# Order of ScalarE's and VectorE's steps at the end of a SwiGLU FFN, in a decoder trunk on one Trainium2 core

## The chip, the cores and the metric

One NeuronCore of a Trainium2 chip runs the whole program. The metric is device time of one launch in microseconds (us). TensorE does the matmuls (PE in the profile), VectorE is DVE, ScalarE is ACT, GpSimd is POOL, SyncE is SP and issues the loads of the weights. Each engine runs its own instructions strictly in the order in which they are written, and waits for others by counting semaphores.

## The reference, cut to what matters

Four layers, each of them FFN, token mixer, FFN: twelve sub-layers, of which eight are FFNs of this form, with 256 tokens, a model width of 1024 and an inner width of 2816, in float32.

```python
def rmsnorm(x, g):
    x32 = x.astype(jnp.float32)
    y = x32 * lax.rsqrt(jnp.mean(x32 * x32, axis=-1, keepdims=True) + EPS)
    return (y * g.astype(jnp.float32)).astype(x.dtype)

def swiglu(x, wg, wu, wd):
    return (jax.nn.silu(x @ wg) * (x @ wu)) @ wd
...
        x = x + 0.5 * rmsnorm(swiglu(rmsnorm(x, g[0]), ffn1_wg[i], ffn1_wu[i], ffn1_wd[i]), g[1])
```

## The kernel before, in words

**Weights come as a stream of pieces** of 128 x 2048 floats (1 MB), in the order of their use. A piece passes through four hands. SP loads it into one of three buffers `raw` (L580). ScalarE's `high` (L1254) rounds it to the matmul's format in `w_high`, one of six places. VectorE's `low` (L1702) subtracts that from the piece and so makes the rest, `w_low`. TensorE then multiplies in three passes: high by high, high by low, low by high. The three `raw` buffers tie the end of this line to its beginning: SP loads piece p only when `low` of piece p - 3 is done. It waits for `piece_split`, a semaphore that `low` raises, so the order of VectorE's `low` steps is the order and the time of the loads.

**An FFN** has 33 pieces, w0 to w0 + 32, where w0 is its first. The inner width is 22 blocks of 128. For a block TensorE makes gate and up products (`block`), ScalarE makes silu of the gate (`silu_of`, L1300), and VectorE multiplies it by up (`times_up`, L1775). The down projection works in chunks of two blocks. Chunks 0 to 8 are done with seven products in place of eight (`seven`), which need sums of the result to be put together at the end. Chunks 9 and 10 (blocks 18 to 21) are done plainly (`chunk`). Pieces w0 + 29 and w0 + 30 hold the weights of blocks 20 and 21, w0 + 31 and w0 + 32 those of chunks 9 and 10. Pieces from w0 + 33 on belong to the next sub-layer. The constants are BLOCKS = 22, SEVENS = 9, FFN_PIECES = 33, CHUNKS = 11.

**TensorE's order at the end of an FFN**: block 19, the last of the seven products of chunk 8 (L774 to L778), block 20, block 21, then chunk 9 for the first 128 tokens, chunk 10 for the first 128 tokens, and after that the second 128 tokens with two groups of transposes of the next sub-layer's input among them (L649). Block 20 waits until block 19 has been multiplied by `times_up`; block 21 until `first_part_out` (L1343) has copied a partial output out of its bank; chunk 9 until `join` and `chunk_low` are done; chunk 10 until `h_low` of block 21 (L1866) is done; the transposes wait for the normalised input, xn (L1750).

**ScalarE's order there**: `high(w0 + 30)`, silu of block 18, `high(w0 + 31)`, `high(w0 + 32)`, silu of block 19, `first_part_out`, `chunk_high` (L1337), `high` of w0 + 33 and w0 + 34, silu of block 20, `h_high` of it (L1348), `high(w0 + 35)`, silu of block 21, `h_high` of it, `high(w0 + 36)`, then the squares of the output for the norm (`square_y`, L1263).

**VectorE's order there**: `times_up` of block 18, `low` of w0 + 30 and w0 + 31, `times_up` of block 19, `low(w0 + 32)`, `join` (L1849 to L1855, five additions that put the partial outputs together; they need ScalarE's `first_part_out`), `low(w0 + 33)`, `times_up` of block 20, `chunk_low` (L1841), `h_low` of block 20, `low(w0 + 34)`, `times_up` of block 21, `join_second`, `h_low` of block 21, `join_second`, `low(w0 + 35)`, then the joint between sub-layers: `gain_y` (L1721), `update_x` (L1738), `pre_norm` (L1750).

At the end of the eighth and last FFN no further pieces follow, so `high` and `low` of w0 + 33 and up do nothing there.

Of the kernel before, what the change touches and what calls it, by code (L numbers as in the profile page):

```python
# [163 lines left out]
def build(nc, x_in, gains, first_gain, stream, gate_w, gate_b, conv_k, ident_in, rope_in, att_mask_in, ml_mask_in,  # L164
          tri_in, out):
    with ExitStack() as ctx:
# [18 lines left out]
        def high_of(p):  # L185
            return w_high[:, p % RING, place(p)]
# [240 lines left out]
        def w_of(sub):  # L427
            return BASE[sub]

        def ffn_no(sub):  # L430
            return KINDS[:sub].count("ffn")
# [37 lines left out]
        def half_of(c, first, last):  # L469

            return slice((c % 2) * 1024 + first * P, (c % 2) * 1024 + last * P)

        def free_part(sub, c):

            return w_of(sub) + down_piece(c) + 1
# [764 lines left out]
        def _(act):  # L1240
# [5 lines left out]
            def high(p, turn=0):  # L1246

                if p >= PIECES:
                    return
                act.wait_ge(raw_landed[p % RAW], 16 * (p // RAW + 1) + 32 * turn)  # L1250
                if p >= RING:

                    act.wait_ge(piece_used, p - RING + 1 + RING * turn)
                nc.scalar.activation(high_of(p)[:, :], raw[:, p % RAW, :], ACT.Copy).then_inc(piece_high, 1)  # L1254
# [78 lines left out]
            def chunk_high(sub, c):  # L1333

                act.wait_ge(h_ready, BLOCKS * ffn_no(sub) + 2 * c + 2)
                act.wait_ge(piece_used, free_part(sub, c - 2))
                nc.scalar.activation(oT_hi_flat[:, half_of(c, 0, 4)], h_all[:, c % 2, 0:4, :].rearrange("p a b -> p (a b)"),  # L1337
                                     ACT.Copy).then_inc(hT_high_done, 1)

            def first_part_out(sub):  # L1340

                act.wait_ge(piece_used, free_part(sub, SEVENS - 1))
                nc.scalar.activation(sums[:, 0:HALF], ps[:, 1, :], ACT.Copy).then_inc(first_copied, 1)  # L1343
# [88 lines left out]
            def ffn(sub):  # L1432
                w0 = w_of(sub)

                def unit(c, turn=0):
                    p = w0 + block_piece(2 * c + 2)
                    silu_of(sub, 2 * c + 2, turn=turn)
                    high(p + 4, turn)
                    corners_high(sub, c + 1, turn)
                    silu_of(sub, 2 * c + 3, turn=turn)  # L1440
                    sums_high(sub, c + 1, turn)
                    seven_h_high(sub, c + 1, turn)
                    high(p + 6, turn)

                silu_of(sub, 1)
                if sub == 0:
                    high(w0 + 4)
                corners_high(sub, 0)
                if sub == 0:
                    silu_of(sub, 2)  # L1450
                sums_high(sub, 0)
                high(w0 + 6)
                if sub:
                    silu_of(sub, 2)
                silu_of(sub, 3)
                copy_hT(sub, 0)
                seven_h_high(sub, 0)
                corners_high(sub, 1)
                silu_of(sub, 4)
                copy_hT(sub, 1)  # L1460
                sums_high(sub, 1)
                seven_h_high(sub, 1)
                high(w0 + 8)
                if sub == 0:
                    load_gains(sub)
                high(w0 + 9)
                silu_of(sub, 5)
                seven_h_high(sub, 2)
                corners_high(sub, 2)
                sums_high(sub, 2)  # L1470
                high(w0 + 11)
                with act.Fori(0, (SEVENS - 3) // 2) as turn:
                    unit(2, turn)
                    unit(3, turn)
                high(w0 + 30)
                silu_of(sub, BLOCKS - 4)
                high(w0 + 31)
                high(w0 + 32)
                silu_of(sub, BLOCKS - 3)
                first_part_out(sub)  # L1480
                chunk_high(sub, SEVENS)
                high(w0 + FFN_PIECES)
                high(w0 + FFN_PIECES + 1)
                silu_of(sub, BLOCKS - 2)
                h_high(sub, BLOCKS - 2)
                high(w0 + FFN_PIECES + 2)
                silu_of(sub, BLOCKS - 1)
                h_high(sub, BLOCKS - 1)
                high(w0 + FFN_PIECES + 3)
# [203 lines left out]
        def _(dve):  # L1693
# [3 lines left out]
            def low(p, turn=0):  # L1697

                if p >= PIECES:
                    return  # L1700
                dve.wait_ge(piece_high, p + 1 + RING * turn)
                nc.vector.tensor_tensor(low_of(p)[:, :], raw[:, p % RAW, :], high_of(p)[:, :],  # L1702
                                        ALU.subtract).then_inc(piece_split, 1)
# [66 lines left out]
            def times_up(sub, i, turn=0):  # L1770
                dve.wait_ge(silu_done, BLOCKS * ffn_no(sub) + i + 1 + 4 * turn)
                if i >= EARLY:

                    dve.wait_ge(hT_split, H_SPLITS * ffn_no(sub) + i // 2 - 1 + 2 * turn)
                nc.vector.tensor_tensor(h_of(i) if i >= EARLY else h[:, i % 2, :], silu[:, i % 2, :],  # L1775
                                        ps[:, gu_bank(i), SEQ:2 * SEQ], ALU.mult).then_inc(h_ready, 1)
# [168 lines left out]
            def ffn(sub):  # L1945
                w0 = w_of(sub)

                def unit(c, turn=0):
                    p = w0 + block_piece(2 * c + 2)
                    times_up(sub, 2 * c + 2, turn)  # L1950
                    low(p + 3, turn)
                    low(p + 4, turn)
                    sum_w(sub, c + 1, turn)
                    times_up(sub, 2 * c + 3, turn)
                    sum_h(sub, c + 1, turn)
                    corners_low(sub, c + 1, turn)
                    seven_h_low(sub, c + 1, turn)
                    if c == SEVENS - 2:
                        last_sums_low(sub, 0)
                        low(w0 + 29)  # L1960
                        last_sums_low(sub, 1)
                    else:
                        sums_low(sub, c + 1, turn)

                times_up(sub, 1)
                if sub == 0:
                    low(w0 + 4)
                sum_w(sub, 0)
                corners_low(sub, 0)
                if sub == 0:  # L1970
                    times_up(sub, 2)
                sums_low(sub, 0)
                if sub:
                    low(w0 + 6)
                    times_up(sub, 2)
                times_up(sub, 3)
                sum_h(sub, 0)
                if sub == 0:
                    sum_w(sub, 1, steps=(0,))
                    seven_h_low(sub, 0)  # L1980
                    low(w0 + 6)
                    sum_w(sub, 1, steps=(1,))
                else:
                    sum_w(sub, 1, steps=(0,))
                    seven_h_low(sub, 0)
                    sum_w(sub, 1, steps=(1,))
                times_up(sub, 4)
                sum_h(sub, 1)
                corners_low(sub, 1)
                seven_h_low(sub, 1)  # L1990
                sums_low(sub, 1)
                low(w0 + 8)
                low(w0 + 9)
                times_up(sub, 5)
                sum_h(sub, 2)
                sum_w(sub, 2, steps=(0,))
                seven_h_low(sub, 2)
                sum_w(sub, 2, steps=(1,))
                corners_low(sub, 2)
                sums_low(sub, 2)  # L2000
                with dve.Fori(0, (SEVENS - 5) // 2) as turn:
                    unit(2, turn)
                    unit(3, turn)
                unit(SEVENS - 3)
                unit(SEVENS - 2)
                times_up(sub, BLOCKS - 4)
                low(w0 + 30)
                low(w0 + 31)
                times_up(sub, BLOCKS - 3)
                low(w0 + 32)  # L2010
                join(sub)
                low(w0 + FFN_PIECES)
                times_up(sub, BLOCKS - 2)
                chunk_low(sub, SEVENS)
                h_low(sub, BLOCKS - 2)
                low(w0 + FFN_PIECES + 1)
                times_up(sub, BLOCKS - 1)
                join_second(sub, 0)
                h_low(sub, BLOCKS - 1)
                join_second(sub, 1)  # L2020
                low(w0 + FFN_PIECES + 2)
# [392 lines left out]
```

## Time and profile before

| | |
|---|---|
| median of 3 runs | 1978.14 us (1977.76 to 1978.75) |
| the profiled execution | 1979.76 us, of which 1977.3 us is the span from the first to the last instruction |
| PE busy | 1968.9 us (100%) |
| DVE busy | 1619.7 us (82%) |
| ACT busy | 1103.5 us (56%) |
| POOL busy | 26.6 us (1%) |
| loads of `raw` | 353, mostly of 1 MB; DMA queue 1 is busy for 51.3% of 16 engines' span |
| mean granted TensorE clock | 1.0 of full speed |

A busy share is a mean over the whole program. Matmuls are pipelined, so the distance from start to start tells more of TensorE's pace than the length of one. In a timeline each row has the start and the length in us, the engine, the line, the operation and its tiles, and in brackets the engine's idle time before it and what ended it. A row with x2 has two instructions of the same kind one behind the other.

### The profile page before, as it was taken

What the parts mean: (1) busy time and instruction counts of PE and PEld (TensorE: products, weight loads), DVE (VectorE), ACT (ScalarE), POOL (GpSimd) and SP (SyncE); (2) the same over time, 40 slices, a digit from 0 to 9 for tenths busy, and PEclk for the clock granted to TensorE, in tenths of its full rate; (3) what the DMA queues carried; (4) which work ended last, traced back from release to release, by engine and by line L of the source; (5) the groups of instructions that cost most, each with busy time, mean ns of one, the idle gap of its engine ahead of it and who ended that gap; (6) DMA issues with size and microseconds to landing.
All of it is one profiled execution on the core that took longest, in us unless ns stands there. A gap on an engine that the chain in (4) does not pass through costs nothing.

```text
span 1977.3 us, 36362 instructions
## 1 busy us (share of the span) xinstructions
PE 1968.9 (100%) x14818; PEld 1837.9 (93%) x14818; DVE 1619.7 (82%) x1865; ACT 1103.5 (56%) x1208; POOL 26.6 (1%) x52
## 2 busy tenths in 40 slices
PE   9999999999999999999999999999999999999998
PEld 8999989998999999988998999998999899998998
DVE  8988678888888787769898888657888888777886
ACT  6555445555555665666555555645555555545553
POOL 0000000000000000000000000000000000000000
PEclk9999999999999999999999999999999999999999
DMA  7655645564555544435555456534556556554552
GB/s 262 240 211 205 231 171 192 191 239 166 206 212 200 210 175 164 155 131 196 213 202 208 187 198 248 208 134 151 212 193 233 173 209 225 212 184 159 213 191 107
DMA packets 56290, 386.37 MB, mean 195 GB/s; under 512 B 6752, under 2 KB 7136, under 8 KB 11232
## 3 DMA queue, kind: packets, MB, share of 16 engines
q1 hardware_dynamic: 52128, 371.87, 51.3%
q10 hardware_dynamic: 4032, 12.59, 2.0%
q8 instruction: 103, 1.69, 0.3%
q14 instruction: 27, 0.22, 0.0%
HBM read 383.39 MB, written 1.05 MB: 194 GB/s over the span
## 4 chain that ended last, share of the span: by engine, by line
PE 95%; DVE 2%; DMA 1%; issue 1%; ACT 0%; POOL 0%; SPq 0%; DVEq 0%; POOLq 0%; ACTq 0%
PE ps L600 21%; PE ps L601 21%; PE ps L602 21%; PE ps L614 6%; PE ps L615 6%; PE ps L616 6%; PE ps L630 2%; PE ps L627 2%; PE ps L633 2%; PE ps L778 1%; PE ps L774 1%; PE ps L775 1%; PE ps L649 1%; DMA raw<-stream 1%; DVE w_low L1702 1%
## 5 line engine op out<-in xcount | busy, mean ns | idle before, releaser
L1702 DVE TENSOR_TENSOR w_low<-raw,w_high 128x2048 fp32r<-128x2048 f32 x272 | 616.1, 2285 | 84.0 <-ACT w_high L1254 84.0
L600 PE MATMUL ps<-xT_both,w_high 128*128 128x256 f32 x2304 | 638.3, 277 | 0.7 <-DVE region L1775 0.7
L601 PE MATMUL ps<-xT_both,w_high 128*128 128x256 f32 x2304 | 636.9, 276 | 0.0
L602 PE MATMUL ps<-xT_both,w_low 128*128 128x256 f32 x2304 | 636.4, 276 | 0.0
L1254 ACT ACTIVATE w_high<-raw 128x2048 fp32r<-128x2048 f32 x279 | 530.7, 1912 | 45.2 <-DMA raw<-stream 32.5
L600 PEld LDWEIGHTS ps<-xT_both,w_high 128*128 128x128 f32 x2304 | 432.5, 188 | 1.1 <-DVE region L1775 0.6
L601 PEld LDWEIGHTS ps<-xT_both,w_high 128*128 128x128 f32 x2304 | 433.1, 188 | 0.0
L602 PEld LDWEIGHTS ps<-xT_both,w_low 128*128 128x128 f32 x2304 | 432.7, 188 | 0.0
L1300 ACT ACTIVATE region<-ps 128x256 f32<-128x256 f32 x176 | 67.4, 383 | 433.5 <-PE ps L602 426.2
L614 PE MATMUL ps<-xT_both,w_high 128*128 128x256 f32 x726 | 202.5, 279 | 0.0
L615 PE MATMUL ps<-xT_both,w_low 128*128 128x256 f32 x726 | 201.3, 277 | 0.0
L616 PE MATMUL ps<-xT_both,w_high 128*128 128x256 f32 x726 | 201.3, 277 | 0.0
L1775 DVE TENSOR_TENSOR region<-region,ps 128x256 f32<-128x256 f32 x176 | 73.7, 419 | 131.1 <-ACT region L1300 128.6
L600 PE MATMUL ps<-w_high,oT_hi 128*128 128x512 f32 x456 | 178.9, 392 | 0.0
L601 PE MATMUL ps<-w_low,oT_hi 128*128 128x512 f32 x456 | 177.9, 390 | 0.0
L602 PE MATMUL ps<-w_high,oT_lo 128*128 128x512 f32 x456 | 177.8, 390 | 0.0
L1331 ACT ACTIVATE w_high<-xn 128x2048 fp32r<-128x2048 f32 x72 | 138.3, 1920 | 28.5 <-DVE xn L1815 24.5
L1828 DVE TENSOR_TENSOR w_low<-xn,w_high 128x2048 fp32r<-128x2048 f32 x64 | 146.3, 2286 | 4.8 <-ACT w_high L1331 4.8
L614 PEld LDWEIGHTS ps<-xT_both,w_high 128*128 128x128 f32 x726 | 136.5, 188 | 0.6
L616 PEld LDWEIGHTS ps<-xT_both,w_high 128*128 128x128 f32 x726 | 136.6, 188 | 0.0
L615 PEld LDWEIGHTS ps<-xT_both,w_low 128*128 128x128 f32 x726 | 136.5, 188 | 0.0
L1821 DVE TENSOR_TENSOR corner<-raw,corner 128x1536 fp32r<-128x1536 f32 x72 | 126.1, 1751 | 0.0
(242 smaller groups left out, 3143.5 us busy)
## 6 DMA issues: line engine op xcount, KB each, us to landing
raw<-stream SPq DMA_DIRECT2D x351, 1024.0 KB, 4.8
gain<-gains ACTq DMA_DIRECT2D x23, 512.0 KB, 4.8
x<-x_in SPq DMA_DIRECT2D x2, 512.0 KB, 4.3
raw<-stream SPq DMA_DIRECT2D x2, 512.0 KB, 6.4
region<-rope_in SPq DMA_DIRECT2D x1, 512.0 KB, 5.8
out<-x SPq DMA_DIRECT2D x1, 512.0 KB, 2.6
att_mask<-att_mask_in SPq DMA_DIRECT2D x1, 320.0 KB, 5.6
out<-x SPq DMA_DIRECT2D x1, 256.0 KB, 2.1
```

Of the source, the lines that this page charges most:

```text
L600: nc.tensor.matmul(acc, lh, rh, start=start, stop=False, skip_group_check=goes_on)
L601: nc.tensor.matmul(acc, lh, rl, start=False, stop=False, skip_group_check=goes_on)
L602: return nc.tensor.matmul(acc, ll, rh, start=False, stop=stop, skip_group_check=goes_on)
L614: nc.tensor.matmul(acc, lh, rh, start=start, stop=False)
L615: nc.tensor.matmul(acc, ll, rh, start=False, stop=False)
L616: return nc.tensor.matmul(acc, lh, rl, start=False, stop=stop)
L1254: nc.scalar.activation(high_of(p)[:, :], raw[:, p % RAW, :], ACT.Copy).then_inc(piece_high, 1)
L1331: nc.scalar.activation(high_of(p)[:, :], sums, ACT.Copy).then_inc(piece_high, 1)
L1702: nc.vector.tensor_tensor(low_of(p)[:, :], raw[:, p % RAW, :], high_of(p)[:, :], ALU.subtract).then_inc(piece_split, 1)
L1775: nc.vector.tensor_tensor(h_of(i) if i >= EARLY else h[:, i % 2, :], silu[:, i % 2, :], ps[:, gu_bank(i), SEQ:2 * SEQ], ALU.mult).then_inc ...
L1821: nc.vector.tensor_tensor(corner[:, c % 2, 1, :], raw[:, p % RAW, HALF:4 * HALF], corner[:, c % 2, 0, :], ALU.subtract).then_inc(piece_spl ...
L1828: nc.vector.tensor_tensor(low_of(p)[:, :], sums, high_of(p)[:, :], ALU.subtract).then_inc(sums_split, 1)
```

## The change

ScalarE makes `high(w0 + 32)` behind silu of block 19 and `first_part_out` instead of ahead of them. VectorE makes `low(w0 + 32)` behind `join` instead of ahead of it. (The product of block 19, `times_up(sub, BLOCKS - 3)`, stands where it stood.) It applies to all eight FFNs. Nothing is added or removed.

```diff
@@ -1475,9 +1475,9 @@
                 high(w0 + 30)
                 silu_of(sub, BLOCKS - 4)
                 high(w0 + 31)
-                high(w0 + 32)
                 silu_of(sub, BLOCKS - 3)
                 first_part_out(sub)
+                high(w0 + 32)
                 chunk_high(sub, SEVENS)
                 high(w0 + FFN_PIECES)
                 high(w0 + FFN_PIECES + 1)
@@ -2007,8 +2007,8 @@
                 low(w0 + 30)
                 low(w0 + 31)
                 times_up(sub, BLOCKS - 3)
+                join(sub)
                 low(w0 + 32)
-                join(sub)
                 low(w0 + FFN_PIECES)
                 times_up(sub, BLOCKS - 2)
                 chunk_low(sub, SEVENS)
```

## Rows read from the trace of the kernel before

**Rows 1.** The page's chain of work that ended last, shares of the span by engine.

```profile
PE 95%; DVE 2%; DMA 1%; issue 1%; ACT 0%; POOL 0%; SPq 0%; DVEq 0%; POOLq 0%; ACTq 0%
```

**Rows 2.** Timeline of ACT, end of the sixth FFN: start, length, engine, line, tiles.

```profile
1499.31 1.92 ACT L1254 ACTIVATE w_high<-raw 128x2048 fp32r<-128x2048 f32 x1 [2.64 <-DMA raw<-stream]
1501.83 0.38 ACT L1300 ACTIVATE region<-ps 128x256 f32<-128x256 f32 x1 [0.59 <-PE ps L602]
1503.21 0.60 ACT L1343 ACTIVATE xn<-ps 128x512 f32<-128x512 f32 x1 [1.00 <-PE ps L778]
1503.70 0.62 ACT L1337 ACTIVATE oT_hi<-region 128x512 fp32r<-128x512 f32 x1
1504.22 3.71 ACT L1254 ACTIVATE w_high<-raw 128x2048 fp32r<-128x2048 f32 x2
...
1511.00 1.91 ACT L1254 ACTIVATE w_high<-raw 128x2048 fp32r<-128x2048 f32 x1
1514.11 0.38 ACT L1300 ACTIVATE region<-ps 128x256 f32<-128x256 f32 x1 [1.20 <-PE ps L602]
...
1518.20 0.60 ACT L1263 ACTIVATE xn<-ps 128x512 f32<-128x512 f32 x1 [0.97 <-PE ps L602]
```

**Rows 3.** Timeline of DVE, the same stretch.

```profile
1502.58 2.28 DVE L1702 TENSOR_TENSOR w_low<-raw,w_high 128x2048 fp32r<-128x2048 f32 x1
1504.78 0.68 DVE L1849 TENSOR_TENSOR xn<-ps,xn 128x512 f32<-128x512 f32 x1
...
1508.03 2.28 DVE L1702 TENSOR_TENSOR w_low<-raw,w_high 128x2048 fp32r<-128x2048 f32 x1
1510.23 0.41 DVE L1775 TENSOR_TENSOR region<-region,ps 128x256 f32<-128x256 f32 x1
...
1514.52 0.42 DVE L1775 TENSOR_TENSOR region<-region,ps 128x256 f32<-128x256 f32 x1 [0.74 <-ACT region L1300]
...
1515.46 0.41 DVE L1866 TENSOR_TENSOR oT_lo<-region,oT_hi 128x256 fp32r<-128x256 f32 x1
...
1516.39 2.28 DVE L1702 TENSOR_TENSOR w_low<-raw,w_high 128x2048 fp32r<-128x2048 f32 x1
1518.92 0.15 DVE L1721 TENSOR_SCALAR mean_first<-mean_y 128x1 f32<-128x1 f32 x1 [0.25 <-ACT xn L1263]
...
1524.50 1.41 DVE L1750 SCALAR_TENSOR_TENSOR xn<-x,rstd_x,gain 128x512 f32<-128x512 f32 x2 [0.66 <-POOL rstd_x L2301]
```

**Rows 4.** Timeline of SP at that end: the issue of the load of piece w0 + 35.

```profile
1505.03 0.33 SPq L580 DMA_DIRECT2D raw<-stream  x1
```

**Rows 5.** Line L580: issue to landing, us: all 339, then two ends' piece w0 + 35.

```profile
DMA to landing us min/median/max: 4.6/4.8/8.9
...
DMA to landing us min/median/max: 7.0/7.0/7.0
...
DMA to landing us min/median/max: 7.3/7.3/7.3
```

**Rows 6.** Timeline of PE: first matmul of chunk 9, of chunk 10, first transposes.

```profile
1513.91 0.39 PE L600 MATMUL ps<-w_high,oT_hi 128*128 128x512 f32 x1
...
1516.64 0.39 PE L600 MATMUL ps<-w_high,oT_hi 128*128 128x512 f32 x1
...
1525.49 0.60 PE L649 MATMUL ps<-ident,xn 128*128 128x128 f32 x4
```

**Rows 7.** Timeline of ACT at the end of the seventh FFN.

```profile
1677.72 1.92 ACT L1254 ACTIVATE w_high<-raw 128x2048 fp32r<-128x2048 f32 x1 [4.18 <-DMA raw<-stream]
1679.55 0.36 ACT L1300 ACTIVATE region<-ps 128x256 f32<-128x256 f32 x1
```

**Rows 8.** Timeline of PE at the same place.

```profile
1679.67 0.40 PE L778 MATMUL ps<-w_high,oT_lo 128*128 128x256 f32 x2
1680.42 0.38 PE L600 MATMUL ps<-xT_both,w_high 128*128 128x256 f32 x1 [0.36 <-DVE region L1775]
```

**Rows 9.** Busy by stretch: PE, PEld, DVE, ACT, POOL; PE clock; DMA share, GB/s.

```profile
1679.78:1680.42 0.64, 0.28 (x3) 0.08 (x2) 0.48 (x2) 0.45 (x2) 0.00 (x0) 1.00 0.81 333
```

## The prediction

> **What bounds the kernel now.** I read the chain of waits first: 95% of what ended last is TensorE [rows 1]. So an edit on ScalarE or VectorE can only gain where TensorE waits for them, and it loses the moment it makes TensorE wait. Next I read the timelines of the three engines at an FFN's end. Relative to `first_part_out` the eight ends agree to some hundredths of a us but for late loads, so I work on one, the sixth, and count. At that end high(w0 + 32) starts at 1499.31 and is over at 1501.23, before silu of block 19, which waits for TensorE and starts at 1501.83 [rows 2]. Nothing there is in the way of that silu. Only at the seventh end did the piece land late (ScalarE idle for 4.18 us), so that high(w0 + 32) held the silu up [rows 7]; TensorE started two short matmuls at 1679.67 and the next only at 1680.42. The sixth FFN's pace in chunks is 0.23 us per 512 columns [(1516.64 - 1513.91)/12, rows 6], so two of 256 columns take 0.23 us, and 0.52 us were lost [rows 8]. That is what there is to gain: about 0.5 us, once in eight.
>
> **The change on ScalarE.** Silu of block 19 and `first_part_out` wait for TensorE and don't move at seven ends. high(w0 + 32) takes the slot behind `first_part_out`, which is 0.49 us long [rows 2], so from 1503.70. A `high` is 1.9 us long and takes 1.81 from start to start (3.71 for two, less 1.90), so it ends at 1505.6. chunk_high, high(w0 + 33) and high(w0 + 34) slide by 1.8 us, the last to about 1509.7 and with it silu of block 20; it is done at 1510.0. Nobody is held by that, since VectorE comes to it later, as follows.
>
> **The change on VectorE.** After the product of block 19 it now comes to `join`, which waits for `first_part_out`: end 1503.81 plus 0.05 for the signal, so 1503.86. From the old start of low(w0 + 32) at 1502.58 it stands idle for 1.28 us [rows 2, 3]. `join` takes 3.25 us (1504.78 to 1508.03) [rows 3], so low(w0 + 32) runs from 1507.11 to 1509.39 instead of 1502.58 to 1504.86: **4.53 us later**. low(w0 + 33), the product of block 20, chunk_low, h_low and low(w0 + 34) come 1.28 us later each. The product of block 20 then starts at 1511.51, and chunk_low, next behind it, is over by about 1512.5. Chunk 9 wants it at 1513.91 [rows 6]: covered, with over 1 us left.
>
> **The load queue.** This is the part that moves furthest. SP issues the load of w0 + 35 when low(w0 + 32) is done, at 1505.03, 0.17 behind its end [rows 3, 4]. Now it issues it at 1509.56. From issue to landing it is 4.8 us at the median, 4.6 at least [rows 5], so the piece lands at 1514.36. Before, high(w0 + 35) ran at 1511.00 [rows 2]; now it starts at 1514.39. Silu of block 21 is queued behind it on ScalarE.
>
> By the Trainium skill, page "DMA: Bandwidth & Descriptors", section "Anatomy of one DMA", a transfer takes about 2.0 us plus its bytes over 436 GB/s, an estimate of 4.4 us here; the trace's 4.8 decides. By that rule each of the seven ends would lose 0.4 us less and the total be 2.8 us lower. The same page's section "Rules for kernel authors" says to issue a load early and wait for it late, which speaks against this change.
>
> **TensorE's first stall.** Silu of block 21 starts at 1514.39 + 1.81 = 1516.20 instead of 1514.11 [rows 2]. From there to h_low of block 21 the chain is as before: product 0.41 later, h_low 0.94 after that, 0.41 long [rows 2, 3]. It ends at 1517.96, and TensorE can start chunk 10 at 1518.02. It wants to at 1516.64 [rows 6]: **1.38 us of stall**. What had covered this was 0.7 us between the old end of h_low (1515.87) and that start. The bounds: with the shortest landing (4.6) 1.18 us; with the 7.0 and 7.3 us that this very piece took at two of seven ends [rows 5], 3.6 to 3.9.
>
> **TensorE's second stall.** Behind h_low, low(w0 + 35) starts 0.93 us later (1515.46 to 1516.39), so at 1518.48, and takes 2.2 from start to start, until 1520.69. The norm's first step on VectorE was at 1518.92 and would, with TensorE's 1.38, be ready at 1520.30; it starts at 1520.69, 1.77 later than before [rows 3]. The chain from there to xn moves by 1.77. The first half of xn was ready at about 1525.25 (two overlapped instructions take 1.41, one about 0.75) plus 0.06, and TensorE's transposes came at 1525.49 [rows 3, 6], with 0.18 us to spare. Now xn is ready at 1527.08 and TensorE there at 1526.87: another 0.21 us, together **1.59 us per end**. If nothing of this second part comes, 1.38; if the whole delay of the chain gets through, 1.77. I take 1.59, as the slack of 0.18 is read off rows. TensorE's lost time isn't won back, since it has no other idle time to shrink.
>
> **The last FFN** has no piece w0 + 35. Its silu waits for TensorE alone; its cost is nothing.
>
> **The sum.** 7 x 1.59 = 11.1 us. Late landings pass straight through, since ScalarE waits for this piece now: before, two of seven took 2.2 and 2.5 us more than 4.8 [rows 5], which would be 4.7 us; at none it is 0. I take 3.0. The stall at the seventh end goes: 0.5 less. 11.1 + 3.0 - 0.5 = 13.6. The profiled execution took 1979.76 us, 1.6 above the median of 1978.14, part of which may be that stall. Against the median: **1991.7 us**.
>
> **The rivals.**
>
> *Faster: the cover holds.* The load of w0 + 35 comes in time, and only the gain is left. This is decided by the landing: TensorE isn't held if high(w0 + 35) starts 1.38 us earlier, which needs a landing within 3.4 us of the issue, and the fastest of 339 took 4.6 [rows 5]. For it speaks only that I may have misread what silu of block 21 is queued behind. The price, if late pieces w0 + 32 were as frequent as at all eight ends: 8 x 0.52 = 4.2 us, so 1974.0 us. Chance 4%.
>
> *No change: the wait is hidden after all.* With the cover holding and one late piece in eight it is 0.5 us, 1977.6 us. Against it the same row of landings. Chance 7%.
>
> *Slower by contention.* The load of w0 + 36 is now issued 2.2 us behind that of w0 + 35, while it was 5.4 behind before. If both in flight make every landing as late as the late ones [rows 5], by 2.2 us, it is 7 x 2.2 = 15.4 instead of 3.0: 2004 us. For it: both use the same 16 engines. Against it: late landings are a minority. Chance 9%.
>
> *The forecast*, both stalls at seven ends with landings as mixed as before: 78%.
>
> **How the numbers follow.** This kernel's runs can tell 0.2%, or 4 us, from no change. The low end takes the shortest landing and no second stall: 7 x 1.18 - 0.5 = 7.8, rounded to 1985. The high end is 2002, which is late landings at most ends. Slower by over 0.2%: 78 + 9 + 2 = 89%. Within 0.2%: 7%. Faster: 4%. The range leaves out both light rivals, the falling clock and about half of the contention case, some 17%.
>
> **What would show it.** In the changed kernel's ScalarE timeline high(w0 + 35) should wait for the landing at each of seven ends, starting about 11.2 us behind `first_part_out` instead of 7.8; the load should be issued 6.35 behind it instead of 1.82. VectorE should be idle for 1.2 us ahead of `join`. TensorE should show a wait of about 1.4 us (somewhat less by the profile's idle column, which counts from a matmul's modelled end) for h_low, L1866, ahead of chunk 10, and a small one ahead of the transposes. If high(w0 + 35) doesn't wait, the prediction is wrong at its root. If it waits and TensorE doesn't, the cover of 0.7 us was misread.

## The result, and the profile after

The changed kernel takes 1989.12 us at the median of 6 runs (1987.86 to 1992.94), the kernel before 1978.41 us in the 6 runs beside it (1977.69 to 1978.75). The ratio is 1.0056, with a 95% interval from 1.0046 to 1.0066: slower by 0.56%, or 10.7 us. The profiled execution took 1989.03 us, with a span of 1986.5 us against 1977.3 before. That is 9.2 us and not 10.7, since the profiled execution of the kernel before, 1979.76 us, was 1.35 above the median of the others.

First who TensorE waits for, over the whole span of the changed kernel. The columns are who waited, for what, us in total, times, and the longest.

```profile
PE ps L600 <- DVE oT_lo L1866: 8.4, 7, 1.3
PE ps L596 <- DVE ones L1695: 1.1, 1, 1.1
PE ps L649 <- DVE xn L1747: 0.3, 1, 0.3
```

One row is new: seven waits for `h_low`, 8.4 us. Seven is the number of FFNs that another sub-layer follows. Now the sixth end on ScalarE, to be laid beside [rows 2]:

```profile
1509.05 0.38 ACT L1300 ACTIVATE region<-ps 128x256 f32<-128x256 f32 x1 [5.29 <-PE ps L602]
1510.43 0.60 ACT L1343 ACTIVATE xn<-ps 128x512 f32<-128x512 f32 x1 [1.00 <-PE ps L778]
1510.93 1.91 ACT L1254 ACTIVATE w_high<-raw 128x2048 fp32r<-128x2048 f32 x1
...
1513.26 3.71 ACT L1254 ACTIVATE w_high<-raw 128x2048 fp32r<-128x2048 f32 x2
...
1521.58 1.92 ACT L1254 ACTIVATE w_high<-raw 128x2048 fp32r<-128x2048 f32 x1 [1.99 <-DMA raw<-stream]
1523.40 0.36 ACT L1300 ACTIVATE region<-ps 128x256 f32<-128x256 f32 x1
```

`first_part_out` (L1343) starts at 1510.43. high(w0 + 35) starts 11.15 us behind it instead of 7.79, and it has waited 1.99 us for its landing. Silu of block 21 has no idle time ahead of it any more: before, it waited 1.20 us for TensorE; now it stands behind the `high`. VectorE and SP show why the load is late (compare [rows 3, 4]):

```profile
1511.07 0.69 DVE L1849 TENSOR_TENSOR xn<-ps,xn 128x512 f32<-128x512 f32 x1 [1.18 <-ACT xn L1343]
...
1514.32 4.49 DVE L1702 TENSOR_TENSOR w_low<-raw,w_high 128x2048 fp32r<-128x2048 f32 x2
...
1523.80 0.42 DVE L1775 TENSOR_TENSOR region<-region,ps 128x256 f32<-128x256 f32 x1 [1.52 <-ACT region L1300]
...
1524.73 0.42 DVE L1866 TENSOR_TENSOR oT_lo<-region,oT_hi 128x256 fp32r<-128x256 f32 x1
...
1527.87 0.14 DVE L1721 TENSOR_SCALAR mean_first<-mean_y 128x1 f32<-128x1 f32 x1
```

```profile
1516.77 0.33 SPq L580 DMA_DIRECT2D raw<-stream  x1
```

VectorE is idle for 1.18 us ahead of `join`; low(w0 + 32) starts at 1514.32, and SP issues w0 + 35 at 1516.77, 6.34 us behind `first_part_out` instead of 1.82. What this does on TensorE (compare [rows 6]):

```profile
1523.64 0.39 PE L602 MATMUL ps<-w_high,oT_lo 128*128 128x512 f32 x1
1525.20 0.50 PE L600 MATMUL ps<-w_high,oT_hi 128*128 128x512 f32 x1 [1.18 <-DVE oT_lo L1866]
1525.54 0.39 PE L601 MATMUL ps<-w_low,oT_hi 128*128 128x512 f32 x1
1525.77 0.40 PE L602 MATMUL ps<-w_high,oT_lo 128*128 128x512 f32 x1
...
1533.97 0.39 PE L602 MATMUL ps<-w_high,oT_lo 128*128 128x512 f32 x1
1534.19 0.60 PE L649 MATMUL ps<-ident,xn 128*128 128x128 f32 x4
```

Chunk 10 starts 1.56 us behind the last matmul of chunk 9 where 0.23 is the pace: 1.33 us lost. The bracket shows 1.18, since it counts from a modelled end. The transposes come 23.76 us behind `first_part_out` instead of 22.28, which is 1.48 later. Of the 0.15 us more, 0.11 stands right behind the wait: the first matmul after it takes 0.34 us to the next one instead of 0.23. Ahead of the transposes nothing is lost; they follow the matmul before them by 0.22. Over the seven ends the gap ahead of chunk 10 is 1.49 to 1.65 us, the next one 0.34, and the transposes are 1.39 to 1.60 us later than the 22.28 of an end without a late piece, 10.5 us in all.

The gain is there too. At this same end the load of w0 + 32 took 7.3 us:

```profile
DMA to landing us min/median/max: 7.3/7.3/7.3
```

It landed 0.3 us before silu of block 19 started, and its `high` could not have been over before that silu. Here silu runs at once and block 20 starts without a gap. In the old order, at the seventh end of the kernel before, the load took 6.6 us, silu was 0.83 late, and TensorE lost 0.52 us [rows 7, 8]; after a load of 7.3 us silu would have been 1.56 late, so the loss would have been some 1.2 us, an estimate from these rows.

### The profile page after: what moved, and what is told of

Read it like the earlier page. It is cut to its first block, busy times and chain, and to the rows that moved or that the text cites. A ratio compares the mean times of both kernels' runs of the same rounds, so it can differ in the third digit from the quotient of the medians.

```text
span 1986.5 us, 36362 instructions
## 1 busy us (share of the span) xinstructions
PE 1970.6 (99%) x14818; PEld 1836.9 (92%) x14818; DVE 1618.9 (81%) x1865; ACT 1100.3 (55%) x1208; POOL 26.6 (1%) x52
## 4 chain that ended last, share of the span: by engine, by line
PE 93%; DVE 3%; DMA 2%; ACT 1%; issue 0%; POOL 0%; DVEq 0%; POOLq 0%; SPq 0%
PE ps L600 20%; PE ps L602 20%; PE ps L601 20%; PE ps L614 6%; PE ps L615 6%; PE ps L616 6%; PE ps L630 2%; PE ps L627 2%; PE ps L633 2%; DMA raw<-stream 2%; PE ps L778 2%; PE ps L774 1%; PE ps L775 1%; PE ps L649 1%; DVE w_low L1702 1%; ACT w_high L1254 1%
```

## The experiments

All times stand beside runs of the kernel before on the same chip.

### ScalarE's half alone

```diff
-                high(w0 + 32)
                 silu_of(sub, BLOCKS - 3)
                 first_part_out(sub)
+                high(w0 + 32)
```

> ScalarE's half of the change alone: high(w0 + 32) behind silu of block 19 and first_part_out, VectorE's order as before. Relative to the sixth end of the kernel before: low(w0 + 32) has to wait for high(w0 + 32) and starts at 1505.65 instead of 1502.58, join and all behind it on VectorE come 3.07 us later, the load of w0 + 35 is issued 3.1 us later and lands at 1512.9, in time for ScalarE. Theory (what matters is when h_low of block 21 is ready, by whichever queue): VectorE itself is now the late one. chunk_low ends 0.46 us too late for chunk 9, h_low of block 21 1.1 us more too late for chunk 10, the transposes 0.2: 1.74 us per end, seven ends, 12 us: about 1990. Rival A (only the late load matters): the load is in time, so about 1978.4. Rival B (ScalarE's half is harmless, VectorE's half does all): about 1978.4.

Measured: 1990.06 us against 1978.1 us, ratio 1.0059 (1.0044 to 1.0075). VectorE at the sixth end, where `first_part_out` started at 1511.52:

```profile
1513.96 2.29 DVE L1702 TENSOR_TENSOR w_low<-raw,w_high 128x2048 fp32r<-128x2048 f32 x1 [2.98 <-ACT w_high L1254]
...
1519.42 2.28 DVE L1702 TENSOR_TENSOR w_low<-raw,w_high 128x2048 fp32r<-128x2048 f32 x1
1521.62 0.41 DVE L1775 TENSOR_TENSOR region<-region,ps 128x256 f32<-128x256 f32 x1
```

VectorE waits 2.98 us for `high` and is late from there on. TensorE loses 0.51 us ahead of chunk 9 and 0.91 ahead of chunk 10, and over the seven ends its transposes are 1.68 to 1.77 us late. The load is issued 4.90 us behind `first_part_out` and is in time. So rivals A and B fall: the late load isn't the only way to lose this time, and this half is not harmless without the other. What counts is when h_low of block 21 is ready.

### VectorE's half alone

```diff
+                join(sub)
                 low(w0 + 32)
-                join(sub)
```

> VectorE's half of the change alone: low(w0 + 32) behind join, ScalarE's order as before. Theory: join waits for first_part_out as in the changed kernel, low(w0 + 32) ends at the same time, the load of w0 + 35 is issued at the same time (6.35 us behind first_part_out), and silu of block 21 waits behind high(w0 + 35) in the same way: the same stall of 1.36 us and the same total as the changed kernel, 1989.1, give or take 0.7. Rival B' (the slide of the high steps on ScalarE costs the time): about 1978.4. Between the two, around 1984, if both halves share it.

Measured: 1989.86 us against 1978.1 us, ratio 1.0059 (1.0043 to 1.0074). The load is issued 6.34 us behind `first_part_out` and TensorE's waits are those of the changed kernel:

```profile
PE ps L600 <- DVE oT_lo L1866: 8.4, 7, 1.4
```

So this half alone is enough for the loss of the changed kernel, and the slide of the `high` steps adds nothing to it that these runs can tell: the two medians, 1989.86 and 1989.12, lie closer together than the runs of either kernel.

### The late load apart from VectorE's idle time

```diff
                 nc.vector.tensor_tensor(u[3], ps[:, 5, :], u[1], ALU.add).then_inc(joined, 1)
+                low(w0 + 32)
                 nc.vector.tensor_tensor(u[2], ps[:, 3, :], u[1], ALU.add).then_inc(joined, 1)
```

`low(w0 + 32)` goes from its place ahead of `join` to this one inside it, written out here.

> ScalarE's order as before; VectorE does the first two of join's five additions, then low(w0 + 32), then the other three. VectorE is idle for the same 1.2 us ahead of join as in the changed kernel, and all its steps from low(w0 + 33) on are as late as there (1.28 us). Only low(w0 + 32) is earlier, and with it the load of w0 + 35: issued 4.4 us behind first_part_out instead of 6.35, landing at 9.2. Theory (the late load is the cause): high(w0 + 35) starts about 9.3, silu of block 21 at 11.1 instead of 10.9 before and 13.0 changed, h_low is ready 0.2 us before TensorE asks: no stall, about 1978.4, at most 1979.5. Rival C (VectorE's 1.28 us of idle time is the cause): as the changed kernel, 1989.

Measured: 1978.53 us against 1978.1 us, ratio 1.0003 (0.9994 to 1.0012). VectorE's timeline shows the idle time of the changed kernel, 1.18 us:

```profile
1503.40 0.69 DVE L1849 TENSOR_TENSOR xn<-ps,xn 128x512 f32<-128x512 f32 x1 [1.18 <-ACT xn L1343]
1504.12 0.69 DVE L1851 TENSOR_TENSOR xn<-ps,xn 128x512 f32<-128x512 f32 x1
1504.73 2.28 DVE L1702 TENSOR_TENSOR w_low<-raw,w_high 128x2048 fp32r<-128x2048 f32 x1
```

TensorE's waits over the whole span hold no row for `h_low` (L1867 in this kernel), and its transposes are later than before at two ends only, by 0.2 and 0.3 us. Three additions fewer ahead of one `low`, with a load issued at 4.42 instead of 6.34 us, take the loss away. Rival C falls.

### The load late with no work moved

```diff
-                low(w0 + 32)
+                low(w0 + 32, released=0 if sub + 1 < SUBLAYERS else 1)
                 join(sub)
-                low(w0 + FFN_PIECES)
+                low(w0 + FFN_PIECES, released=2)
```

`released` is by how much `low` raises `piece_split`.

> The kernel before in all its orders, but low(w0 + 32) doesn't raise the count that SP waits for, and low(w0 + 33) raises it by two: the loads of w0 + 35 and w0 + 36 are both issued behind low(w0 + 33), 7.3 us behind first_part_out, w0 + 35's 5.45 us later than before. No engine's work is moved. Theory: with a landing of 4.8 us high(w0 + 35) starts at 12.1, TensorE stalls 2.3 us ahead of chunk 10 and 0.2 ahead of the transposes, at seven ends 17 us: 1995.7. With two loads in flight at once the first may take 5.5 to 7 us, which gives 2000 to 2011. Rivals B' and C (moved work on ScalarE or VectorE is the cause): nothing is moved, 1978.4.

Measured: 2002.4 us against 1978.1 us, ratio 1.0123 (1.0108 to 1.0139).

```profile
PE ps L600 <- DVE oT_lo L1867: 15.6, 7, 2.9
```

The line of `h_low` is L1867 here. The wait is the same and longer, with every engine's order as before: the late load is enough. At six ends the load of w0 + 35 took 4.7 to 4.8 us and at the first 5.6, mostly not the 5.5 to 7 I had allowed for, and the wait alone gives about the 1995.7 of the expectation. The other 6 us have another cause, which the last section tells.

### Silu ahead of the late piece

```diff
-                high(w0 + FFN_PIECES + 2)
                 silu_of(sub, BLOCKS - 1)
                 h_high(sub, BLOCKS - 1)
+                high(w0 + FFN_PIECES + 2)
```

This is made in the changed kernel.

> The changed kernel, with silu and h_high of block 21 taken ahead of high(w0 + 35) on ScalarE. The load of w0 + 35 is as late as in the changed kernel, but nothing of TensorE's next input is queued behind it. Theory: silu of block 21 starts at 10.9 again, h_low is ready at 13.1 behind first_part_out, TensorE asks at 13.4: the stall ahead of chunk 10 (1.36 us per end) is gone. The two high steps now lie right ahead of the squares for the norm, which start at 16.15 instead of 15.0, so the chain to xn is 1.16 late with 0.18 to spare: 0.98 us ahead of the transposes, at seven ends 6.9, less up to 0.5: about 1985. Rival (the late load or VectorE's idle time costs the time wherever silu stands): 1989.

Measured: 1986.01 us against 1978.02 us, ratio 1.0047 (1.0033 to 1.006). ScalarE at the sixth end and TensorE's waits over the span:

```profile
1518.95 0.38 ACT L1300 ACTIVATE region<-ps 128x256 f32<-128x256 f32 x1 [1.74 <-PE ps L602]
...
1520.58 3.70 ACT L1254 ACTIVATE w_high<-raw 128x2048 fp32r<-128x2048 f32 x2
1524.19 0.58 ACT L1263 ACTIVATE xn<-ps 128x512 f32<-128x512 f32 x1
```

```profile
PE ps L649 <- DVE xn L1750: 6.2, 7, 1.6
```

No wait for `h_low` is left. Silu waits for TensorE again, and the two `high` steps stand ahead of the norm's squares (L1263), so that TensorE waits ahead of its transposes and loses 0.83 to 0.84 us at four ends, 1.1 to 1.7 at three where w0 + 36 landed later. The stall moves with the order of ScalarE's queue.

### Only silu ahead

```diff
-                high(w0 + 32)
                 silu_of(sub, BLOCKS - 3)
+                high(w0 + 32)
                 first_part_out(sub)
```

> The kernel before, with only silu of block 19 taken ahead of high(w0 + 32) on ScalarE; first_part_out stays behind it, VectorE's order stays. Theory: low(w0 + 32) starts 1.5 us later and the load of w0 + 35 is issued about 3.3 us behind first_part_out's old place, lands at 8.1 and is in time; h_low of block 21 is ready some hundredths of a us before TensorE asks; the norm's chain is 0.35 late with 0.18 to spare, 0.17 us per end, 1.2 in all, and a late piece w0 + 32 costs nothing any more, 0.5 back: 1979, between 1978 and 1980.5. Rival (any step ahead of high(w0 + 32) costs as the changed kernel does): 1989.

Measured: 1979.65 us against 1978.02 us, ratio 1.0008 (0.9999 to 1.0017). Its profile has no wait for `h_low` (L1866). The interval reaches down to no change; if there is a loss, it is at most 0.17%.

### Three additions ahead of the piece

```diff
                 nc.vector.tensor_tensor(u[2], ps[:, 3, :], u[1], ALU.add).then_inc(joined, 1)
+                low(w0 + 32)
                 dve.wait_ge(joined, n + 3)
```

This is made in the changed kernel, with ScalarE's order as changed; `low(w0 + 32)` goes from its place behind `join` to this one inside it.

> The changed kernel, but VectorE does low(w0 + 32) behind the first three of join's five additions instead of behind all. The idle time ahead of join and all from low(w0 + 33) on are as in the changed kernel; the load of w0 + 35 is issued 5.15 us behind first_part_out (before 1.83, with join split in two 4.42, changed 6.34). Theory: it lands at 9.95, high(w0 + 35) starts at 10.0, silu of block 21 at 11.8, h_low is ready 0.17 us too late, the transposes wait 0.2 more: 0.37 per end, 2.6 in all, less up to 0.5: 1980.5, between 1979.5 and 1981.5. Rival (ScalarE's high(w0 + 32) in its new place costs by itself): 1985 or more.

Measured: 1980.65 us against 1978.02 us, ratio 1.0013 (1.0004 to 1.0022). The longest of its stalls is at the sixth end, where the load took 5.5 us instead of 4.8:

```profile
1514.05 1.92 ACT L1254 ACTIVATE w_high<-raw 128x2048 fp32r<-128x2048 f32 x1 [1.50 <-DMA raw<-stream]
1515.87 0.36 ACT L1300 ACTIVATE region<-ps 128x256 f32<-128x256 f32 x1
```

So both moves together, with `low` behind three of the additions, cost 2.6 us. ScalarE's part costs at most that in its new place: VectorE comes to `low(w0 + 32)` 2.6 us behind the start of `first_part_out` here, when its `high` is over, and doesn't wait for it as it did with ScalarE's half alone.

### The changed kernel again

> The changed kernel once more, on the same chip as the three above. Theory: 1989, with seven waits of 1.2 to 1.3 us for h_low and the granted clock at full in them; an execution in which one landing of w0 + 35 is 2 us late is 2 us longer. If the clock also falls here, as in the run with the held loads, matmuls of 512 columns come 0.43 us apart behind a wait, and the execution is longer by 1 to 2 us for each such end.

Measured: 1989.07 us against 1978.02 us, ratio 1.0058 (1.0045 to 1.0072). Seven waits, 8.9 us in all, the longest 1.6 at the one end where w0 + 35 took 5.2 us. Behind every wait the matmuls are 0.23 us apart again after a first distance of 0.34. At the fifth end w0 + 36 took 6.6 us, and there 0.3 us were lost ahead of the transposes too.

### The held load with silu ahead, and the held load again

The first has both edits, that of the held load and that of silu ahead of the late piece.

> The kernel with the held loads (e4), with silu and h_high of block 21 ahead of high(w0 + 35). The load of w0 + 35 is as late as in e4, later than in the changed kernel. Theory: the stall of 2.3 us ahead of chunk 10 is gone, and with it the fall of the clock. high(w0 + 35) starts at 12.1 and high(w0 + 36), whose load took 7 us there and lands at 15.0, at 15.0; the squares start at 16.85 instead of 15.0, 1.7 us per end ahead of the transposes: 12 us, about 1990, against e4's 2002. Rival (lateness of the load costs the same wherever silu stands): 2002.

Measured: 1992.08 us against 1977.86 us, ratio 1.0069 (1.0052 to 1.0086). The lateness of the load costs 10 us less when silu isn't behind it; some 3 of these are falls of the clock, two in place of four, at the 1.6 us each that the last section finds. What is over the expectation stands at the fourth and fifth ends: w0 + 36 took 8.1 us, TensorE waited 2.3 us for xn, and the clock fell there, against what I expected.

> e4 once more, for the clock. The time is 2000 to 2004 again. If the fall of the clock follows from the length of the wait, some ends of seven show it again after the same wait of 2.3 us, not always the same ones; if it was a chance of one execution, the clock is at full throughout and the time near 1996.

Measured, one run: 2000.97 us against 1977.86 us. The clock fell at four of seven ends, as in the first such run.

### The runs side by side

The issue of w0 + 35 and the first transposes are counted from the start of `first_part_out`, at the third of the eight ends; their times are from the timelines of SP and TensorE.

| kernel | issue of w0 + 35 | transposes | median, us |
|---|---|---|---|
| before | 1.8 | 22.3 | 1978.4 |
| join split behind two additions | 4.4 | 22.3 | 1978.5 |
| join split behind three, ScalarE as changed | 5.0 | 22.5 | 1980.7 |
| ScalarE's half | 4.9 | 24.0 | 1990.1 |
| VectorE's half | 6.3 | 23.7 | 1989.9 |
| changed | 6.3 | 23.8 | 1989.1 |
| changed, silu first | 6.3 | 23.1 | 1986.0 |
| load held | 7.3 | 24.7 | 2002.4 |
| load held, silu first | 7.3 | 23.6 | 1992.1 |

Where silu of block 21 is queued behind `high(w0 + 35)`, a load issued up to 4.4 us behind is free, and most of each further microsecond goes into TensorE's time. ScalarE's half is the exception: its load is in time, and VectorE is late instead. The kernel with only silu ahead isn't in the table, as its `first_part_out` itself stands later. None of these versions beats the kernel before: what there is to win is 0.5 us (for a load of 6.6 us) to some 1.2 (7.3 us) at an end where w0 + 32 comes late, and that was one end in eight in each of the two profiles, before and after.

## Why the prediction was right

Forecast were 1991.7 us and slower; measured is 1989.12, 10.7 over before where 13.6 was forecast.

- **VectorE's idle time and the later `low`.** Forecast 4.53 us later for the load's issue; measured 4.52 (1.82 to 6.34). The ends of `first_part_out`, `join` and two `low` steps could be laid behind one another from rows of before, since nothing in their lengths changed.
- **Landing.** Forecast 4.8 us, measured 4.70 to 4.87 at the seven ends.
- **First stall.** Forecast 1.38 us, measured 1.26 to 1.42 (gaps of 1.49 to 1.65 less 0.23).
- **Second stall.** This term was wrong: forecast 0.21 us ahead of the transposes, measured nothing at six ends and under 0.1 at the first. TensorE comes 0.11 us later than by the first stall alone, by the slow first matmul. And the chain to xn is 1.61 us late where 1.77 was forecast: `pre_norm` starts 22.90 us behind `first_part_out` instead of 21.29. The step passed the delay on undiminished, but before, VectorE had waited 0.1 us for ScalarE's second squares within that chain, and now it doesn't: from the first mean (L1721) to the second (L1725) it is 1.26 us instead of 1.36. With TensorE 0.11 us later and xn 0.16 earlier than forecast, the 0.21 us are covered. The time of the slow first matmul had no term in the sum, so that the two errors, 0.21 too much and 0.11 too little, partly cancel.
- **The last FFN**: no wait, as forecast.
- **The stall at the seventh end** is gone, 0.5 us; the transposes there had come at 22.91 instead of 22.28, so it may have been 0.6.
- **Late landings** were the term that missed by most: 3.0 us forecast, 0 measured in the profiled execution, 0.6 in its repetition. The step took the lateness of w0 + 35 in the kernel before along to its new time. At the fourth end w0 + 33 and w0 + 34 took 7.0 and 7.2 us in the changed kernel too (7.3 and 7.6 before), while w0 + 35, issued 4.5 us later, took 4.8 instead of 7.3. At the third end, where before w0 + 35 alone had been late (7.0), it took 4.85. Why these loads are late no run here shows.

The terms measured give 10.5 - 0.5 = 10.0 us. The spans differ by 9.2; of the rest, 0.6 lies ahead of the first FFN's end, where `first_part_out` starts at 163.51 instead of 164.08 in code that is the same. Most of it is a stall of the kernel before at 62.4 us that the changed kernel's execution didn't have:

```profile
62.44 0.38 PE L600 MATMUL ps<-xT_both,w_high 128*128 128x256 f32 x1 [0.34 <-DVE region L1775]
```

Against the medians 0.7 us are left over, and no term is known for them.

One source in the prediction is applied too widely. The fit behind its estimate of 4.4 us for a load is given by the Trainium skill, page "DMA: Bandwidth & Descriptors", section "Anatomy of one DMA", for transfers issued by GpSimd. These loads are issued by SP, and the 4.8 us of the trace, which the sum went by, held.

Of the rivals, contention shows on the other load: w0 + 36, now 2.2 us behind w0 + 35, took 5.1 to 6.5 us instead of 4.8 to 5.3. It cost under 0.1 us in this execution, since ScalarE got to it later, and 0.3 us at one end of the repetition, where it took 6.6 us. The clock didn't fall in the two profiles of the changed kernel. That the halves each cost as much as both together was not in the prediction: it had called ScalarE's move harmless because VectorE comes later, and that holds only with VectorE's move beside it.

## What to carry to other kernels

With a ring of load buffers, a step that frees a buffer sits at the head of a chain that comes back some pieces later. If it is moved back (here by 4.5 us), look for the step that needs the new load, and for what is queued behind that step on its engine. Spare time has to be read at the far end (here 0.7 us at `h_low` and 0.18 at xn), and an engine with idle time in its profile can still have none at that place.

## What the runs showed of the hardware that was not expected

The granted clock fell around the end of single waits of TensorE. With the held load, at the sixth end, after 2.06 us of idle time (TensorE's timeline, then the stretches, whose last three columns are the clock, the DMA share and GB/s):

```profile
1534.34 0.50 PE L600 MATMUL ps<-w_high,oT_hi 128*128 128x512 f32 x1 [2.06 <-DVE oT_lo L1867]
1534.67 0.39 PE L601 MATMUL ps<-w_low,oT_hi 128*128 128x512 f32 x1
...
1535.89 0.63 PE L600 MATMUL ps<-w_high,oT_hi 128*128 128x512 f32 x1
1536.32 0.63 PE L601 MATMUL ps<-w_low,oT_hi 128*128 128x512 f32 x1
```

```profile
1534.30:1536.00 1.70, 1.66 (x7) 1.34 (x8) 1.70 (x2) 1.30 (x1) 0.00 (x0) 0.93 0.37 154
1536.00:1539.00 3.00, 3.00 (x9) 2.33 (x8) 2.34 (x4) 1.00 (x3) 0.00 (x0) 0.50 0.23 44
1539.00:1545.00 6.00, 6.00 (x28) 4.91 (x27) 4.72 (x8) 2.21 (x6) 1.09 (x2) 0.99 0.37 153
```

